# Attention in one fused block: where the probabilities are summed and what VectorE reads

## The reference

```python
def one_block(qblk):
    s = jnp.einsum('bqhd,bkhd->bhqk', qblk, k).astype(jnp.float32) * scale
    p = jax.nn.softmax(s, axis=-1).astype(v.dtype)
    return jnp.einsum('bhqk,bkhd->bqhd', p, v)
...
y_lat = jnp.concatenate([o_att..., retention_out(y_r, rg, g_ret)], axis=-1) @ w_o
```

## Time and profile before

| what | value |
|---|---|
| median of 3 runs | 2949.53 us (2948.57 to 2950.4) |
| the profiled execution's own time | 2951.48 us |
| its span | 2948.3 us |
| mean clock of TensorE | 0.963 of full |
| TensorE busy | 2743.5 us (93%) |
| VectorE busy | 2098.0 us (71%) |
| ScalarE busy | 1441.9 us (49%) |
| GpSimd busy | 351.1 us (12%) |

### The profile page before, as it was taken

The page is one execution under the profiler, slowest core; times in us unless marked ns, Lnnn a source line. Parts: engine busy times, 40 slices in busy tenths (PEclk is TensorE's granted clock), DMA queues, the critical chain, the costliest instruction groups (busy, mean ns, idle before and its releaser), DMA issues. The chain is left out here.

```text
span 2948.3 us, 51233 instructions
## 1 busy us (share of the span) xinstructions
PE 2743.5 (93%) x20805; PEld 2240.3 (76%) x20805; DVE 2098.0 (71%) x3131; ACT 1441.9 (49%) x2146; POOL 351.1 (12%) x377
## 2 busy tenths in 40 slices
PE   5999999899959999999999988992999999999996
PEld 1877778688857666666666657882899999999995
DVE  3555555677749999999998984457676766767666
ACT  3555555322237667677676652111444444444444
POOL 0111111122210000000000002221010111101102
PEclk8999999899979999999999998995899999999998
DMA  7544443422230110110110005334476777767778
GB/s 247 178 157 151 156 154 110 134 75 78 71 62 3 38 29 13 37 29 13 37 29 13 7 12 204 125 135 141 158 228 200 229 211 229 218 203 228 224 219 309
DMA packets 267072, 375.70 MB, mean 127 GB/s; under 512 B 35571, under 2 KB 186646, under 8 KB 265174
## 3 DMA queue, kind: packets, MB, share of 16 engines
q1 hardware_dynamic: 257334, 337.83, 35.7%
q0 software_dynamic: 9504, 34.61, 5.2%
HBM read 286.61 MB, written 85.77 MB: 126 GB/s over the span
## 5 line engine op out<-in xcount | busy, mean ns | idle before, releaser
L1997 PE MATMUL ebank<-gathered_T,w_gate_up 128*128 128x256 f32 x4608 | 546.9, 280 | 1.4 <-DVE gathered_T L2219 1.4
L1997 PEld LDWEIGHTS ebank<-gathered_T,w_gate_up 128*128 128x128 f32 x4608 | 543.6, 189 | 3.2 <-DVE gathered_T L2219 1.8
L1276 PE MATMUL abank<-head_qT,head_kT 96*128 96x512 f32 x1728 | 410.2, 397 | 17.2 <-DVE head_qT L1385 17.2
L1276 PEld LDWEIGHTS abank<-head_qT,head_kT 96*128 96x128 f32 x1728 | 322.7, 190 | 97.6 <-issue 23.5
L1356 ACT ACTIVATE scores<-scores 128x1536 f32<-128x1536 f32 x192 | 274.3, 1476 | 242.9 <-DVE scores L1415 242.9
L1415 DVE TENSOR_TENSOR scores<-scores,abank 128x1536 f32<-128x1536 f32 x192 | 322.6, 1747 | 43.5 <-PE abank L1296 43.3
L1351 ACT ACTIVATE scores<-abank 128x512 f32<-128x512 f32 x576 | 326.0, 603 | 31.3 <-PE abank L1276 5.6
L498 PE MATMUL bank<-w_in_sb,h_T 128*128 128x512 f32 (+1 forms) x1296 | 292.8, 384 | 9.5 <-DVE h_T L699 9.5
L1306 PE MATMUL abank<-scores,head_v 128*64 128x256 f32 x2304 | 293.8, 390 | 1.2 <-ACT scores L1356 1.2
L2011 PE MATMUL ebank<-w_down,hidden_T 128*128 128x512 f32 x1152 | 281.1, 399 | 2.9 <-DVE w_down L2229 2.6
L498 PEld LDWEIGHTS bank<-w_in_sb,h_T 128*128 128x128 f32 x1296 | 243.8, 191 | 44.5 <-DVE h_T L699 10.1
(11 more groups left out here) (285 smaller groups left out, 3682.4 us busy)
## 6 DMA issues: line engine op xcount, KB each, us to landing
w_gate_up_whole<-in_w_exp_gate SPq DMA_DIRECT2D x48, 1024.0 KB, 6.0
w_gate_up_whole<-in_w_exp_up SPq DMA_DIRECT2D x48, 1024.0 KB, 8.6
w_down_whole<-in_w_exp_down SPq DMA_DIRECT2D x192, 256.0 KB
ada_rest<-in_w_ada SPq DMA_DIRECT2D x16, 1024.0 KB
x_tile<-in_x_all SPq DMA_DIRECT2D x18, 512.0 KB
scratch_h<-h_T_whole SPq DMA_DIRECT2D x18, 512.0 KB
ada_w<-in_w_ada SPq DMA_DIRECT2D x4, 2048.0 KB
chunk_h_T_whole<-scratch_h SPq DMA_DIRECT2D x16, 512.0 KB
```

Of the source, the lines that this page charges most:

```text
L1276: m = pe.matmul(banks[S_BANKS[kt % 4]][:, :], kT[u][:, kp, k], qT[u][:, qp, q], start=(n == 0), stop=(n == 2))
L1997: x = pe.matmul(banks[f % 3][:, j * CAP:(j + 1) * CAP], w_gu[c][:, wp, j, k, o:o + P], xsT[:, xp, k, :], start=(k == 0 and n == 0), stop=( ...
```

## The change

- The sums of the probabilities are no longer taken on TensorE tile by tile. GpSimd adds the probabilities of the 18 tiles in five steps into a tile of three (`prob_sums`), and TensorE multiplies that by 32 columns of ones (`prob_sum`), one block later, after score tile 11 of the next block.
- GpSimd, not VectorE, computes the rest of the split of keys and queries (except for the first head).
- The running maximum lies in PSUM (`max_bank`, the banks of the transposes). It starts from score tiles 0 and 1 in SBUF and tiles 8 and 9 still in their PSUM banks (`held_maximum`), and then takes two tiles at a time. So no operation of VectorE in the loop has two SBUF inputs. TensorE waits at score tile 12 for that first maximum.
- ScalarE copies the undivided output and the sums to SBUF (`raw_output`), SyncE stores both, in three DMAs in place of one.
- The division is done in `mix_out`: SyncE loads the sums of a tile, repeated over 64 partitions, in two DMAs; VectorE takes their reciprocal and multiplies (`scale_att`). ScalarE's `round_mix` waits for it.

```diff
-        v1 = [sb(f"head_v{u}", [P, T, P]) for u in range(2)]
+        v1 = [sb(f"head_v{u}", [P, T, DV]) for u in range(2)]
         sc = [sb(f"scores{u}", [P, T, QB]) for u in range(2)]
-        mx = sb("score_max", [P, G, QB])
+        acc = [sb(f"prob_sums{u}", [P, G, QB]) for u in range(2)]
+        mx = sb("score_max", [P, 2, QB])
         mq = sb("max_cols", [P, 4])
         mrep = mx[:, 1, :].rearrange("p (c n) -> p c n", c=4)
-        o_sb = sb("out_T", [64, QB])
-        inv = sb("sums_inverse", [P, P])
-        banks = [ctx.enter_context(nc.psum_tensor(f"abank{b}", [P, 512], F32)) for b in range(8)]
+        o_sb = sb("out_and_sums", [P, HB + P])
+        ones = sb("ones_32", [P, 32])
+        held = ctx.enter_context(nc.psum_tensor("score_banks", [P, 2, QB], F32))
+        low = [held[:, 0, :], held[:, 1, :], ctx.enter_context(nc.psum_tensor("abank2", [P, 512], F32))]
+        mx_psum = ctx.enter_context(nc.psum_tensor("max_bank", [P, 2, QB], F32))
+        banks = [*low, mx_psum[:, 0, :], mx_psum[:, 1, :],
...
+            def store(head, n, b):
+                sg["raw"].wait(sp, b)
+                settled(sp)
+                for half in range(2):
+                    q = n * QB + half * HB
+                    sp.dma_start(scratch["attT"][bass.ds(head * DV, DV), q:q + HB], o_sb[64 * half:64 * half + 64, 0:HB]).then_inc(sg["out_stored"].sem, 16)
+                q = scratch["att_sum"][bass.ds(head, 1), n * QB:(n + 1) * QB].rearrange("o (c n) -> (o c) n", c=4)
+                sp.dma_start(q, o_sb[0:P:32, HB:]).then_inc(sg["out_stored"].sem, 16)
             for u in range(2):
...
+                if has_before(pair, j):
+                    store(pair * 2 + ((j - 1) // NB), (j - 1) % NB, b - 1)
+                if j % NB == NB - 2 and not final_pair(pair):
...
-                pool.memset(v1[u][:, :, DV:], 1.0).then_inc(ones_set, 1)
+            def split(head, u, n):
+                for i, (x, whole, c) in enumerate(thirds(u, n)):
+                    sg["rounded"].wait(pool, head, 2 * n + i + 1)
+                    pool.tensor_tensor(x[:, 1, c], whole[:, 1, c], x[:, 0, c].bitcast(F32), ALU.subtract).then_inc(sg["rest"].sem, 1)
+            def turn(pair, j, b, more):
+                split_next(split, pair, j)
+                p, a = sc[j % 2], acc[j % 2]
+                sg["probs"].wait(pool, b, 2)
+                sg["out_psum"].wait(pool, b - 2)
+                pool.tensor_tensor(a[:, :, :], p[:, 0:G, :], p[:, G:2 * G, :], ALU.add).then_inc(sg["summed"].sem, 1)
+                for g in range(2, GROUPS):
+                    sg["probs"].wait(pool, b, g + 1)
+                    sg["summed"].wait(pool, b, g - 1)
+                    pool.tensor_tensor(a[:, :, :], a[:, :, :], p[:, g * G:(g + 1) * G, :], ALU.add).then_inc(sg["summed"].sem, 1)
+            pool.memset(ones[:, :], 1.0).then_inc(ones_set, 1)
+            loop(pool, turn)
...
+                if kt == HELD + 4:
+                    sg["max_keys"].wait(pe, b, 1)
...
-                        pe.matmul(ps[64 * half:64 * half + 64, 0:HB], v1[u][:, kt, 0:DV], p[:, kt, half * HB:(half + 1) * HB],
-                                  start=(kt == 0), stop=(kt == T - 1), skip_group_check=True)
-                for kt in range(g * G, (g + 1) * G):
+                        m = pe.matmul(ps[64 * half:64 * half + 64, 0:HB], v1[u][:, kt, :], p[:, kt, half * HB:(half + 1) * HB],
+                                      start=(kt == 0), stop=(kt == T - 1), skip_group_check=True)
+                return m
+            def prob_sum(j, b):
+                ps, a = banks[5 + j % 2], acc[j % 2]
+                sg["summed"].wait(pe, b)
+                for t in range(G):
                     for c in range(4):
-                        m = pe.matmul(ps[32 * c:32 * c + 32, HB:HB + P], v1[u][:, kt, DV:DV + 32], p[:, kt, c * P:(c + 1) * P],
-                                      start=False, stop=(kt == T - 1), skip_group_check=True)
-                return m
+                        m = pe.matmul(ps[32 * c:32 * c + 32, HB:HB + P], ones[:, :], a[:, t, c * P:(c + 1) * P],
+                                      start=False, stop=(t == G - 1), skip_group_check=True)
+                m.then_inc(sg["out_psum"].sem, 1)
...
+                        if kt == HELD + 3 and has_before(pair, j):
+                            prob_sum((j - 1) % 2, b - 1)
...
+                    if not more and g == 3:
+                        prob_sum((j - 1) % 2, b - 1)
+                m.then_inc(sg["valued"].sem, 1)
...
+                sg["summed"].wait(act, b - 2, max(g, 1))
...
+            def raw_output(j, b):
+                sg["out_psum"].wait(act, b)
+                sg["out_stored"].wait(act, b - 1)
+                act.activation(o_sb[:, :], banks[5 + j % 2][:, 0:HB + P], ACT.Copy).then_inc(sg["raw"].sem, 1)
...
+                    if has_before(pair, j):
+                        raw_output((j - 1) % 2, b - 1)
                     round_next(split, pair, j)
...
-            def maximum(j, b, g):
-                s = sc[j % 2]
-                sg["scores"].wait(dve, b, (g + 1) * G)
-                if g == 1:
-                    sg["max_psum"].wait(dve, b - 1)
-                    dve.tensor_tensor(mx[:, :, :], s[:, 0:G, :], s[:, G:2 * G, :], ALU.max).then_inc(sg["max_keys"].sem, 1)
-                else:
-                    sg["max_keys"].wait(dve, b, g - 1)
-                    dve.tensor_tensor(mx[:, :, :], mx[:, :, :], s[:, g * G:(g + 1) * G, :], ALU.max).then_inc(sg["max_keys"].sem, 1)
-            def fold(b):
-                for g in (1, 2):
-                    sg["max_keys"].wait(dve, b, GROUPS - 2 + g)
-                    dve.tensor_tensor(mx[:, 0, :], mx[:, 0, :], mx[:, g, :], ALU.max).then_inc(sg["max_keys"].sem, 1)
+            def held_maximum(j, b):
+                sg["scores"].wait(dve, b, HELD + 2)
+                sg["max_psum"].wait(dve, b - 1)
+                sg["shifted"].wait(dve, b - 1)
+                dve.tensor_tensor(mx_psum[:, :, :], sc[j % 2][:, 0:2, :], held[:, :, :], ALU.max).then_inc(sg["max_keys"].sem, 1)
+            def maximum(j, b, i):
+                n = PAIRS_LATER[i]
+                sg["scores"].wait(dve, b, 2 * n + 2)
+                sg["max_keys"].wait(dve, b, i + 1)
+                dve.tensor_tensor(mx_psum[:, :, :], sc[j % 2][:, 2 * n:2 * n + 2, :], mx_psum[:, :, :], ALU.max).then_inc(sg["max_keys"].sem, 1)
+            def fold(j, b):
...
+            def fold(j, b):
+                s, done = sc[j % 2], len(PAIRS_LATER) + 1
+                sg["scores"].wait(dve, b, T)
+                sg["max_keys"].wait(dve, b, done)
+                dve.tensor_tensor(mx[:, 0, :], s[:, T - 2, :], mx_psum[:, 0, :], ALU.max).then_inc(sg["max_keys"].sem, 1)
+                dve.tensor_tensor(mx_psum[:, 1, :], s[:, T - 1, :], mx_psum[:, 1, :], ALU.max).then_inc(sg["max_keys"].sem, 1)
+                sg["max_keys"].wait(dve, b, done + 2)
+                dve.tensor_tensor(mx[:, 0, :], mx[:, 0, :], mx_psum[:, 1, :], ALU.max).then_inc(sg["max_keys"].sem, 1)
+            def keys_maximum(j, b):
+                held_maximum(j, b)
+                for i in range(len(PAIRS_LATER)):
+                    maximum(j, b, i)
...
-                dve.tensor_copy(mrep, last(mq[:, :], P)).then_inc(sg["max_rep"].sem, 1)
+                dve.tensor_tensor(mrep, rows, last(mq[:, :], P), ALU.max).then_inc(sg["max_rep"].sem, 1)
...
-            def output(j, b):
-                ps = banks[5 + j % 2]
-                sg["out_psum"].wait(dve, b)
-                sg["out_stored"].wait(dve, b - 1)
-                dve.reciprocal(inv[:, :], ps[:, HB:HB + P]).then_inc(sg["out"].sem, 1)
-                sg["out"].wait(dve, b, 1)
-                for c in range(4):
-                    for d in (0, 32):
-                        r = 64 * (c // 2) + d
-                        x = dve.tensor_tensor(o_sb[d:d + 32, c * P:(c + 1) * P], ps[r:r + 32, c % 2 * P:(c % 2 + 1) * P],
-                                              inv[32 * c:32 * c + 32, :], ALU.mult)
-                x.then_inc(sg["out"].sem, 1)
...
+                for w in range(2):
+                    heads = scratch["att_sum"].rearrange("(o k w) n -> w o k n", o=1, w=2)[w, :, :, bass.ds(token, P)]
+                    sp.dma_start(sums[u][64 * w:64 * w + 64, :, :], heads.to_broadcast([64, KH, P])).then_inc(att_loaded.sems[u], 32)
...
-                att_loaded.wait(act, m, u)
+                sg["att_scaled"].wait(act, m)
...
+            def scale_att(m, u):
+                att_loaded.wait(dve, m, u)
+                settled(dve)
+                x = mt_whole[u][:, 1, 0:KH, :]
+                dve.reciprocal(sums[u][:, :, :], sums[u][:, :, :]).then_inc(sg["att_scaled"].sem, 1)
+                sg["att_scaled"].wait(dve, m, 1)
+                dve.tensor_tensor(x, x, sums[u][:, :, :], ALU.mult).then_inc(sg["att_scaled"].sem, 1)
...
+                if ahead:
+                    scale_att(m + 2, u)
```

(9 more changed lines are left out.)

65 lines of the change are left out of this document (31 added, 34 removed).

## The result

The kernel after takes 2960.51 us (median of 6 runs, 2960.27 to 2963.84), the one before beside it 2949.97 (6 runs, 2948.57 to 2952.14). The ratio is 1.0039, 95% interval 1.0027 to 1.0051: 0.4% slower, where 0.7% faster was forecast. The profiled execution has a span of 2958.6 us and a mean clock of 0.953 (before: 2948.3).

What follows compares the result with a forecast made beforehand. TensorE was taken to set the attention period, VectorE a microsecond behind, and TensorE the projection's tiles. From 2951.5 us, attention -45 and projection +24 gave 2930.5, stated as 2930, 0.7% less; range 2900 to 2990.

Steps and rivals of the forecast that it cites:

- The circle in attention: Attention block: chain of subtractions, maxima, folds, transposes and value groups sets 25.8 us a block, gain 1.4; 31 blocks take 800.
- PSUM: Attention rival: VectorE reading and writing the same PSUM bank costs extra; 2955, or 3180 if doubled; chance 0.12.
- GpSimd: Attention rival: GpSimd hinders VectorE or sets the period, 28 us a block, 3000 us; chance 0.08.
- The rival Clock: Attention rival: TensorE's idle times lower its clock, costing 1.6 us a block, +50, 2980 us; chance 0.16.
- GpSimd's adds: Attention: five adds a block at 3.45 us each, hidden up to 4.1 an add; stage end about 31 us.
- 14.75 a tile: Output projection: chain of 29.5 us for two tiles, 1.2 a tile more than now; fourteen tiles cost 17 to 20.
- Landing: Projection chain: from a tile's sum with x to its loaded data, 7.0 us, sums landing about 1 us behind.
- the collision: Projection: GpSimd's two-input work beside VectorE's addition makes the added cost 1.4 us a tile instead of 1.2.
- The head: Start of the projection: division work and four more DMAs ahead of the weights, nothing to 10 us, taken as 5.5.
- The projection takes it all: Projection rival: clock and collisions there make +45 or more, 2950 us; chance 0.07.
- upper bound of 35 us for the tiles: Projection: most that the fourteen tiles would cost, with landing 2 us later and all collisions.
- The projection hides it: Projection rival: VectorE has half of a tile free, so the division is hidden, 2908 us; chance 0.12.

Runs made afterwards that it cites:

- one add: Kernel after without division in the projection, GpSimd making only the first of its five adds in a block; 2894.49 us.
- the division and no new loads: Kernel after, VectorE still inverting and multiplying in every tile, but sums loaded once for the first two tiles and not again; 2936.77 us.
- filler matmuls: Kernel after plus 16 matmuls into an unused bank ahead of TensorE's wait for each even projection tile from 2 on; 2947.77 us.
- without division: Kernel after with sums neither loaded, inverted nor multiplied in during the projection, attention output left undivided; 2904.22 us, ratio to before 0.9854.
- sums loaded only: Kernel after with the sums loaded and ScalarE waiting for them, but VectorE neither inverting nor multiplying; 2914.98 us.
- sums early: Kernel after, sums of tile m + 3 loaded at turn m, those of m + 2 inverted while VectorE waits for the reciprocal root; 2909.64 us.
- retention half first: Kernel after, ScalarE and GpSimd handling a tile's retention half, which needs no division, before waiting for its attention half; 2942.84 us.

## Why the prediction was wrong

- **The circle in attention: right.** 25.8 forecast, 25.72 measured. The first maximum came 10.28 us after the subtractions began (10.45), the later ones at 1.229 (1.225). That the 31 blocks took 800.5 us for 800 is partly luck: the block is 0.08 shorter than forecast, and four longer blocks (25.98 to 27.72) make that good. The rivals PSUM and GpSimd in the blocks are out. The rival Clock came true in one block of 31, which took 2.0 us more.
- **GpSimd's adds: right.** 3.49 for 3.45, hidden (one add shows the same block), 30.2 us at the tail for 31. Why VectorE must not read two SBUF tiles was only half seen. The earlier trace rows gave twice the time; it is over five times for a short operation.
- **The failed step: "14.75 a tile", and the 17 to 20 us made of it for 14 tiles.** They cost 46.4. The chain was the right one, but two tiles were put at 29.5 us and took 34.15. TensorE's start to the sum: 14.95 forecast, 17.43 measured (the low clock). Landing: 7.0, and 8.18; the text gave the sums 1 us behind the tile, the sum of terms used 0.7, and it was 1.9. VectorE: 4.13, and 4.08. ScalarE and GpSimd: 3.4, and 4.46 (the collision, for which the forecast added 0.2 a tile). The largest part, 2.48 of 4.65 us, is the clock, which the sum put at nothing. Yet the forecast's 29.5 contained an idle TensorE of 29.5 - 27.2 = 2.3 us in one place, next to the 2.58 us of the earlier trace rows after which the clock had fallen; with the division and no new loads it did fall after 2.34. The clock was weighed for the blocks, and for the projection only in a rival of 0.07. A fallen clock lengthens the chain, but not the idle time, so it repeats in every second tile. The filler matmuls, which touch only that, gave back 14 us.
- **The head: mis-sized too.** 5.5 us forecast and 10.9 measured. The first tile's sum with x stands at 35.5 us from the stage's first DMA, 6.1 later than before, and the second 4.8 later again. The first delay is mostly the loads' (6.0 us between the kernels without division and with the sums loaded only), the second comes with VectorE's work (0.6 with the sums loaded only, 2.4 with the division and no new loads).
- **The rivals.** "The projection takes it all", at +45 or more and 0.07, is what happened, for its named reason; its size was 57. The upper bound of 35 us for the tiles did not hold, since it left out the clock: without the clock's 17.6 the 46.4 would be 29. "The projection hides it" is nearly what the version with the sums early does (2909.6 against 2908), though its projection is still 6 us longer than before, at the head.

## What to carry to other kernels

Before a division (or any step) is moved to another stage, write out that stage's chain from the release of a buffer to the next use of it, and put in it only what must stand behind the landing: the reciprocal did not have to. Compare each idle time of TensorE that your own forecast creates with those in the trace that did and did not lower its clock. Between 1.8 and 2.9 us both happened here, so a forecast that lands there needs both times. In this kernel the adds on GpSimd beside VectorE were free only as long as VectorE's operations there read one SBUF tile, so the two changes belong together.

## What the runs showed of the hardware

- VectorE's maximum of 1024 elements with the running maximum in PSUM, read and written in the same banks, takes 1229 ns beside a working GpSimd, and the mean is the same where GpSimd makes one add of five; an addition of 1024 from SBUF took 1225.
- With two SBUF tiles beside GpSimd's adds of 3.5 us, 512 elements took 3.79 us instead of 0.69, and the adds 4.31 instead of 3.49.
- TensorE's clock, by the idle time before it: after 3.95 to 7.08 us it was at 0.50 (kernel after). It fell after 2.00 us in a block of attention, after 2.34 and 2.64 (division, sums not loaded again), 2.94 (sums loaded only) and 1.82 (retention half first, tile 10). It stayed at 1 after 2.02 us in a block of the kernel with the sums early, after 1.97 (retention half first) and after 2.94 (division, sums not loaded again, last tile). So the length of one idle time did not decide it between 1.8 and 2.9 us. The waits of 1.07 and 1.16 us in each block and of 1.44 in the projection left it at 1.
- VectorE's reciprocal takes 3.35 us for 512 elements, five times the multiplication of 512 (0.69), and 0.95 for 128.
